# Expert rows of a mixture-of-experts kernel: the gate weight moved to VectorE, the sums moved into adding DMA writes, the last block and all biases joined by one product

## The reference

```python
h2 = rmsnorm(x, norm_ffn_g)                        # [512, 1024]
logits = h2 @ w_router + b_router                  # 32 experts
topv, idx = top_k(logits, 4); gates = softmax(topv)
# for every (token, chosen expert) pair:
gu  = h2[token] @ w_gate_up[e] + b_gate_up[e]      # [2048]
act = (clip(up) + 1) * (gate * sigmoid(1.702 * gate))
y   = act @ w_down[e] + b_down[e]                  # [1024]
x   = x + sum over the token's 4 experts of gates * y
# second block, first lines:
xn = rmsnorm(x, pre_g[0]); proj = xn @ w_in[0]
```

## Time and profile before

| what | us |
|---|---|
| median of 3 runs | 3075.31 (3072.84 to 3075.5) |
| the profiled execution's own time | 3074.51 |
| its span in the trace | 3072.7 |
| TensorE busy | 2839.8 (92%) |
| VectorE, ScalarE, GpSimd busy | 1196.2, 802.5, 116.7 |
| expert stage, first product to last copy of y | 723.55 to 1757.37 |

### The profile page before, as it was taken

The page is one execution under the profiler, slowest core; times in us unless marked ns, Lnnn a source line. Parts: engine busy times, 40 slices in busy tenths (PEclk is TensorE's granted clock), DMA queues, the critical chain, the costliest instruction groups (busy, mean ns, idle before and its releaser), DMA issues.

```text
span 3072.7 us, 42784 instructions
## 1 busy us (share of the span) xinstructions
PE 2839.8 (92%) x15464; PEld 1695.2 (55%) x15465; DVE 1196.2 (39%) x2551; ACT 802.5 (26%) x1607; POOL 116.7 (4%) x132
## 2 busy tenths in 40 slices
PE   8989889998999989899889779999999999999999
PEld 7874567753333333233333368575676596676774
DVE  6770674323212222122221166435333355444432
ACT  3221661111322222222222223423111224323111
POOL 0000100000000000000000000011000000110000
PEclk9999999997999999999999989999999999999999
DMA  4222002237999999999999552021321331122221
GB/s 175 83 69 69 15 1 96 83 138 298 395 419 401 425 426 403 418 395 411 423 406 397 205 200 97 28 93 36 102 83 55 99 101 55 54 74 76 82 69 69
DMA packets 119627, 578.08 MB, mean 188 GB/s; under 512 B 13933, under 2 KB 19437, under 8 KB 85712
## 3 DMA queue, kind: packets, MB, share of 16 engines
q1 hardware_dynamic: 110000, 559.37, 46.9%
q0 software_dynamic: 9504, 17.07, 1.5%
HBM read 572.97 MB, written 20.97 MB: 193 GB/s over the span
## 4 chain that ended last, share of the span: by engine, by line
PE 79%; DMA 11%; DVE 5%; ACT 2%; issue 2%; DVEq 1%; POOLq 0%; ACTq 0%; SPq 0%
PE banks L399 28%; PE banks L1547 11%; DMA arena<-in_w_up 10%; PE banks L336 8%; PE banks L1088 7%; PE banks L1588 5%; PE banks L841 4%; PE banks L1555 3%; PE banks L819 3%; PE banks L854 2%; PE banks L830 2%; PE banks L1594 2%; PE banks L275 1%; DVE arena L907 1%; PE banks L1527 1%
## 5 line engine op out<-in xcount | busy, mean ns | idle before, releaser
L399 PE MATMUL banks<-arena 128*128 128x256 f32 (+2 forms) x4256 | 916.3, 376 | 18.4 <-ACT arena L436 7.9
L399 PEld LDWEIGHTS banks<-arena 128*128 128x128 f32 x4256 | 795.7, 191 | 128.6 <-issue 21.9
L1547 PE MATMUL banks<-arena 128*64 128x512 f32 x2048 | 476.3, 610 | 67.8 <-DMA arena<-in_w_up 49.8
L1547 PEld LDWEIGHTS banks<-arena 128*64 128x64 f32 x2048 | 154.3, 139 | 343.8 <-issue 341.7
L436 ACT ACTIVATE arena<-banks 128x512 f32<-128x512 f32 (+2 forms) x152 | 89.1, 587 | 622.2 <-PE banks L399 622.2
L336 PE MATMUL banks<-arena 128*128 128x512 f32 x576 | 250.0, 592 | 0.0
L1588 PE MATMUL banks<-arena 128*64 128x512 f32 x1024 | 236.1, 599 | 0.0
L1689 DVE TENSOR_TENSOR arena<-banks,arena 128x512 f32<-128x512 f32 x64 | 44.3, 692 | 486.6 <-PE banks L1573 261.3
L452 DVE TENSOR_TENSOR arena<-banks,arena 128x512 f32<-128x512 f32 (+2 forms) x114 | 77.3, 678 | 383.2 <-PE banks L399 381.7
L1088 PE MATMUL banks<-arena 128*128 128x512 f32 x512 | 222.9, 592 | 3.7 <-DVEq L205 3.7
L384 DVE TENSOR_TENSOR arena<-arena 128x1024 f32<-128x1024 f32 (+2 forms) x152 | 182.4, 1200 | 21.8 <-issue 19.4
(11 more groups left out here) (218 smaller groups left out, 2389.1 us busy)
## 6 DMA issues: line engine op xcount, KB each, us to landing
arena<-in_w_up SPq DMA_DIRECT2D x128, 2048.0 KB, 23.4
arena<-in_w_down SPq DMA_DIRECT2D x128, 1024.0 KB, 21.5
arena<-in_w_in SPq DMA_DIRECT2D x76, 1024.0 KB, 5.0
arena<-in_w_out SPq DMA_DIRECT2D x12, 1024.0 KB, 5.0
arena<-in_w_branch SPq DMA_DIRECT2D x24, 512.0 KB, 4.7
arena<-expert_rows SPq DMA_DIRECT2D x4, 2048.0 KB, 14.5
arena<-in_w_in SPq DMA_DIRECT2D x2, 2048.0 KB, 10.0
arena<-in_w_in SPq DMA_DIRECT2D x4, 832.0 KB, 4.4
```

The lines of the kernel that those rows point to most:

```text
L399: last = PE.matmul(PS[:, bank, t * width:(t + 1) * width], one[:, t * P:(t + 1) * P], other, start=(first and t == 0 and kk == 0), stop=(t ...
L1547: last = PE.matmul(PS[HB * s:HB * (s + 1), 4 + h], xT[:, k, 0:HB], gate_up(2 * h + s, k), start=(k == 0), stop=(k == 7))
```

## The change

1. The row lists keep only tokens. 16 more products (L1337 of the changed kernel) build `GLIST`, the gate weight of each row of each block, from 16 small ScalarE activations (`gate_rows`).
2. In each block but the last VectorE multiplies `y` by the weights in place (L1745) once ScalarE has written it, and only then releases the scatter. The scatter goes to `x_sums` (XD) in DRAM, one row for each token, with `compute_op=ADD`: the transfer adds the rows to what stands there. SP has filled `x_sums` with x, 2 MB, in the router stage.
3. The last block isn't scattered. VectorE runs it outside its loop. `y` stands in rows 0 to 95 of a tile and `b_down` in rows 96 to 127. A matching left side `SEL` has in rows 0 to 95 a 1-of-512 selection by token times the gate, and in rows 96 to 127 the transposed gates. So 8 products of 512 columns (L1640) give the last block's share and all down biases for all tokens at once. The 8 bias products in the router stage and the four additions behind them are gone.
4. SP loads `x_sums` back into x, 2 MB, while the last block is at work. The combine stage has no fence and one addition for each tile (L1794). The weights of the second block's first product wait only for the last block's activations. ScalarE loads the table for Sqrt with a small activation at the end of its expert loop. TensorE reads `few` (short or long block) ahead of a wait instead of behind it.

```diff
+        XD = nc.dram_tensor("x_sums", [S, D], F32, kind="Internal").ap()
@@ router stage, PE
                 for tt in range(TT):
-                    last = PE.transpose(PS[0:NE, 3, tt * P:(tt + 1) * P], Gm[:, tt], ident)
+                    last = PE.matmul(PS[BS:P, 3, tt * P:(tt + 1) * P], Gm[:, tt], ident, start=True, stop=True, tile_position=(0, BS))
                 last.then_inc(SEM["gt_mm"], 1)
-                pe.wait_ge(SEM["gt_rdy"], up(1))
-                pe.wait_ge(SEM["bdown_in"], 16)
-                down_biases(0, 4)
-                down_biases(1, 6)
...
-                down_biases(2, 2)
-                pe.wait_ge(SEM["table_rdy"], up(1))
-                down_biases(3, 0)
+                for a_ in range(16):
+                    if a_ % 4 == 0:
+                        pe.wait_ge(SEM["gate_rows"], up(a_ // 4 + 1))
+                    last = PE.matmul(PS[0:BS, 2, 0:LISTS], gate_rows[:, a_], slots[:, a_].rearrange("p b e -> p (b e)"),
+                                     start=(a_ == 0), stop=(a_ == 15))
+                last.then_inc(SEM["gates_listed"], 1)
@@ router stage, ACT
+                    for a_ in range(4 * tt, 4 * tt + 4):
+                        last = AC.activation(gate_rows[:, a_], rows_at[:, a_, 0:BS], ACT.Copy, scale=per_slot[:, a_:a_ + 1])
@@ router stage, DVE and SP
+                dve.wait_ge(SEM["gates_listed"], up(1))
+                V.tensor_copy(v(GLIST, LISTS, BS), PS[0:BS, 2, 0:LISTS])
+                V.drain().then_inc(SEM["gates_out"], 1)
...
+                sp.dma_start(XD.rearrange("(t p) d -> p t d", p=P), x3).then_inc(SEM["sums_in"], 16)
@@ expert stage, SP
                 sp.wait_ge(SEM["all_out"], up(1))
+                for tt in range(TT):
+                    sp.dma_start(x3[:, tt], XD[tt * P:(tt + 1) * P, :]).then_inc(SEM[f"comb{tt}"], 16)
+                sp.wait_ge(SEM["act_rdy"], up(2 * final + 2))
@@ expert stage, PE
-                pe.wait_ge(SEM["bias_added"], up(2))
                 gather_T(1)
-                pe.wait_ge(SEM["bias_added"], up(4))
-                with pe.Fori(0, nb) as j:
+                pe.wait_ge(SEM["gt_rdy"], up(1))
+                pe.wait_ge(SEM["gates_out"], up(1))
+                with pe.Fori(0, final + 1) as j:
+                    few = entry(pe, FEW, j, 1)
                     pe.wait_ge(SEM["xt_free"], up(j + 1))
...
+                pe.wait_ge(SEM["y_rdy"], up(final + 1))
...
+                for tt in range(TT):
+                    for n in range(2):
+                        last = PE.matmul(PS[:, SUMS[tt] + n], v(SEL + P * tt, P), v(Y_ + 512 * n, 512), start=True, stop=True)
+                    last.then_inc(SEM["comb_mm"], 1)
@@ expert stage, DVE
-                    V.tensor_tensor(x3[:, tt], x3[:, tt], PS[:, (4, 6, 2, 0)[tt]:(4, 6, 2, 0)[tt] + 2].rearrange("p a b -> p (a b)"),
-                                    ALU.add).then_inc(SEM["bias_added"], 1)
...
-                    V.tensor_copy(rsc, column(ALLR, here)).then_inc(SEM["rsc_rdy"], 1)
+                    if not ends:
+                        dve.wait_ge(SEM["rows_out"], up(j))
...
+                        V.tensor_copy(rsc, column(ALLT, here))
+                        dve.wait_ge(SEM["y_rdy"], up(j + 1))
...
+                        V.tensor_scalar(v(Y_, D, BS), v(Y_, D, BS), AR[0:BS, bass.ds(here + GLIST, 1)], None, ALU.mult)
+                        V.drain().then_inc(SEM["rsc_rdy"], 1)
@@ expert stage, POOL
-                    pool.wait_ge(SEM["y_rdy"], up(n))
...
                     pool.wait_ge(SEM["rsc_rdy"], up(n))
...
-                    G.indirect_dma_start(out=YD, out_offset=bass.IndirectOffsetOnAxis(ap=rsc.bitcast(U32), axis=0),
-                                         in_=y, in_offset=None,
-                                         bounds_check=S * TOPK - 1, oob_is_err=False).then_inc(SEM["scattered"], 16)
+                    G.indirect_dma_start(out=XD, out_offset=bass.IndirectOffsetOnAxis(ap=rsc.bitcast(U32), axis=0),
+                                         in_=y, in_offset=None, bounds_check=S - 1, oob_is_err=False,
+                                         compute_op=ALU.add).then_inc(SEM["scattered"], 16)
@@ combine stage
-                    sp.dma_start(v(BIG + 4096 * tt, 4096),
-                                 YD[tt * 512:(tt + 1) * 512, :].rearrange("(p k) d -> p (k d)", k=4)).then_inc(
-                                     SEM[f"comb{tt}"], 16)
...
-                    for k in range(4):
-                        last = V.scalar_tensor_tensor(x3[:, tt], v(BIG + 4096 * tt + D * k, D), v(GATES + 4 * tt + k, 1),
-                                                      x3[:, tt], ALU.mult, ALU.add)
-                        if k < 3:
-                            V.drain()
+                    dve.wait_ge(SEM["comb_mm"], up(tt + 1))
+                    last = V.tensor_tensor(x3[:, tt], x3[:, tt], PS[:, SUMS[tt]:SUMS[tt] + 2].rearrange("p a b -> p (a b)"), ALU.add)
```

More of the change, by code:

```diff
@@ L1275, in weights_in @@
             sp.dma_start(to, src).then_inc(SEM[f"ch{u}"], 16)
-        def down_biases(tt, bank):
-            for n in range(2):
-                last = PE.matmul(PS[:, bank + n], v(GT + tt * P, P, NE), v(BD + n * 512, 512, NE), start=True, stop=True)
-            last.then_inc(SEM["fin_mm"], 1)
         def gather(pool, n):
@@ L1626, in copy_T @@
                     AC.activation(v(XT, D), PS[:, 4:6].rearrange("p a b -> p (a b)"), ACT.Copy).then_inc(SEM["xt_free"], 1)
+                act.wait_ge(SEM["gates_listed"], up(1))
                 copy_T(1)
-                with act.Fori(0, nb) as j:
+                with act.Fori(0, final + 1) as j:
                     few = entry(act, FEW, j, 1)
@@ L1671, in dve_ @@
                 dve.wait_ge(SEM["gathered"], 16)
                 V.tensor_copy(tok, column(ALLT, entry(dve, BCOL, 1, LISTS - 1))).then_inc(SEM["tok_rdy"], 1)
-                with dve.Fori(0, nb) as j:
+                here_last = entry(dve, BCOL, final, LISTS - 1)
+                V.tensor_copy(v(TOKF, 1, BS), column(ALLT, here_last)[0:BS])
+                V.tensor_copy(v(TOKF + 5, 1, BS), AR[0:BS, bass.ds(here_last + GLIST, 1)])
+                V.drain()
+                for tt in range(TT):
+                    V.tensor_scalar(v(TOKF + 1 + tt, 1, BS), v(TOKF, 1, BS), float(PART), float(-P * PART * tt), ALU.mult, ALU.add)
@@ L1674, in dve_, with block @@
+                V.drain()
+                for tt in range(TT):
+                    last = V.tensor_scalar(v(SEL + P * tt, P, BS), v(CO["iota_p"], P, BS), v(TOKF + 1 + tt, 1, BS), v(TOKF + 5, 1, BS),
+                                           ALU.is_equal, ALU.mult)
+                last.then_inc(SEM["sel_made"], 1)
+                def block(j, ends):
                     e = entry(dve, BE, j, NE - 1)
-                    here = entry(dve, BCOL, j, LISTS - 1)
-                    after = entry(dve, BCOL, j + 2, LISTS - 1)
@@ L1677, in dve_ @@
                     V.tensor_copy(v(BCUR, 16), dyn(BT + e * 16, 16))
-                    dve.wait_ge(SEM["gathered"], 16 * j + 32)
-                    apart(dve, 16 * j + 32)
-                    V.tensor_copy(tok, column(ALLT, after))
-                    V.drain().then_inc(SEM["tok_rdy"], 1)
+                    if ends:
+                        V.drain()
+                    else:
+                        here = entry(dve, BCOL, j, LISTS - 1)
+                        after = entry(dve, BCOL, j + 2, LISTS - 1)
+                        dve.wait_ge(SEM["gathered"], 16 * j + 32)
+                        apart(dve, 16 * j + 32)
+                        V.tensor_copy(tok, column(ALLT, after))
+                        V.drain().then_inc(SEM["tok_rdy"], 1)
@@ L1732, in pool_ @@
                 next_rows(3)
+                pool.wait_ge(SEM["sums_in"], 16)
                 scatter(1)
-                with pool.Fori(1, nb) as j:
+                with pool.Fori(1, final) as j:
                     next_rows(j + 3)
```

75 lines of the change are left out of this document (43 added, 32 removed).

## The result

The changed kernel takes 3088.1 us (median of 6 runs, 3085.68 to 3092.48), the kernel before 3075.4 in the same runs: 1.0042 times as long, 95% interval 1.0030 to 1.0055. The prediction was 3062 and faster; the change made the kernel slower. The profiled execution took 3087.68 us, 13.2 more than the 3074.51 of before.

The account below looks back on a forecast made before the run. In the expert stage transfers set the pace in three stretches, TensorE elsewhere. 3074.5 − 23 (seam behind) + 10 (adding scatter) + 0 (seam ahead) = 3061.5, and 0.8 more is 3062 us; range 3050 to 3077.

Parts of the forecast that it names:

- The seam behind: From the last copy of `y` to TensorE's continuous work in the combine stage: a gain of 23 us, bounds 19 to 25.
- The multiplication and its waits: Expert loop: VectorE's multiplication of `y` and the later scatter fit into 8.1 us of cover, so cost nothing.
- Landings (rival 3): Expert loop, short blocks: scatter landings beyond some 25 us become the stall; 3112 us at a landing of 30; chance 0.09.
- The seam ahead: Router stage up to the first expert product: small gains and delays, sum 0, from −2 to +7 us.
- The adding scatter: Expert loop: an adding row costs twice a plain one, 23 us of engine time, 0.44 of it paid: 10 us.
- three saturated stretches: Parts of the expert stage with full DMA share where transfers set the pace: 450 us, 0.44 of the stage.
- The upper bound of 20 us: Expert loop, adding scatter: an adding row at three times the plain price, 46 × 0.44 = 20 us.
- rival 2: Expert loop: an adding row costs three to five times a plain one, 20 to 40 us, total 3072 to 3092; chance 0.14.

Follow-up runs that it names:

- experiment 2: The changed kernel with VectorE's multiplication of `y` and its wait taken out, adding write kept: 3088.55 us, 1.0045 of the kernel before.
- e1: The changed kernel with a plain write in place of the adding one in the scatter to `x_sums`, so the sums are lost: 3053.57 us.
- e4: The same run as experiment 2: the changed kernel without VectorE's multiplication of `y` and its wait, adding write kept: 3088.55 us.
- experiments 5 to 10: Kernel before plus 64 scratch rows a block at chosen partitions (four runs, the last 3097.09 us); gather turned by 64 partitions, kernel before 3055.64, changed kernel 3060.84.

## Why the prediction was wrong, by its own steps

- **The seam behind: right.** 24.1 us for 23, and the parts too: additions of 1.22 us for 1.2, the first of them 4.1 us after the last copy of `y` for 3.5, continuous work after 22.1 us for 23. The sixteen records took 8.81 us: the first four come about 0.86 apart, then the rest 0.43, where the prediction had three of them slow.
- **The multiplication and its waits: right.** Nothing, by experiment 2.
- **Landings (rival 3): refuted.** 13.5 us at most.
- **The seam ahead: 0 predicted, +1.6 measured,** in the range, of two parts that partly cancel: first gather issued 2.3 us earlier, and the write of `x_sums` held it for about 4 (1 predicted, 6 at worst). The +1.6 itself is not clear of the spread: in e1 and e4, which have the same steps there, the first product starts at 724.88 and 723.36, where the kernel before has 723.55. That the two parts nearly cancel is luck.
- **The adding scatter: this step failed, +10 predicted, +35 measured.** Its price for a row was right: 327 ns for 159. The two source reads that the prediction cites from the Trainium skill, "Collectives: The Full Stack", on why ReduceScatter is half of AllGather, would double a row's price, and the trace agrees with 2.06. Its two other factors, the mean over the engines and the share of the stage in which it is paid, were too small. "23 us of engine time over the stage" (20.8 by the packets) is a mean over 16 engines, but 64 rows lie on eight; on those it is up to 31 × 8 × 0.168 = 42 us. And "of that only what falls in the three saturated stretches is paid, 0.44 × 23" took the windows with a share of 1.0 for all of the stage in which transfers count; 35 of 42 is 0.84. Long blocks paid as well, eight of them by 1.1 to 5.5 us each, in a stage for which the earlier trace rows has a share of 0.98 from end to end. One of them, from 842.73 to 879.21 in the kernel before, lies outside all three windows and has a share of 1.01 at 426 GB/s, though TensorE is busy for 35.0 of its 36.5 us; it takes 2.0 us more in the changed kernel. So the prediction's "elsewhere TensorE sets the pace and a transfer more costs nothing" doesn't hold there. The first factor is shown by experiments 5 to 10. The second is only read from the periods; no run isolates it, and 5.2 us in the eight long blocks are TensorE's longer busy time, for which the prediction had no term.
- **The upper bound of 20 us** and rival 2 were drawn as multiples of the same mean. Rival 2's time (3072 to 3092) holds the result, but by luck: its reason was a row of three to five times the price, and a row costs 2.06.

What stays open: why a 96-partition layout slowed the stream by 13 us in the stage before (1021.1 for 1008.3, in an execution of 3088.08, the fastest of its four), in which the weight packets themselves took longer; and why the turned gather brought back 20 us of the total for 24 of the stage.

## What to carry to other kernels

Cost a small transfer beside a saturated stream by its most loaded DMA engine, not by bytes over 16: rows that lie on partitions 0 to 63 alone load half of the engines with twice the mean, and in this kernel two small products were enough to move them. The page's DMA share doesn't show such an imbalance: it is 0.99 to 1.00 after the change as before. With a DMA share of 0.98 and TensorE near its own limit, 0.84 of the load added to the most loaded engine was paid here (35 of 42 us), and 0.6 of the load taken off it came back (24.3 of 32 × 8 × 0.16 = 41). And before a sum is moved into the writes, ask what it competes with: here the adding writes took 35 us of a stream that was full, and a plain write with an early read back got within 4 us of what free additions would give (3057.6 and 3053.6).

## What was not expected of the hardware

- Partitions decide: 64 extra rows a block cost 35.3, 37.7, −1.5 or 16.6 us of the stage by their partitions alone.
- Turning a gather's 64 rows to the other half of the partitions gave 20 us in a kernel in which gathers and scatters together take 1.5% of the DMA engines' time.
- GpSimd is busy for 1591 ns with an adding scatter and for 1008 with a plain one.
- A plain 4 KB row packet takes 160 ns in the mean when its own transfer has 128 partitions, and 188 or 172 ns when it has 96, beside the same weight stream.
